# Two matmul orders for a split-weight projection unit: by turns, or all high weights and then all low weights

## The reference

```python
def conv_ffn(h, w_in, conv_w, conv_b, w_out):          # layers 0 and 1, D_FF = 2816
    z = h @ w_in                                       # (256 x 1024) @ (1024 x 5632)
    u, g = z[..., :D_FF], z[..., D_FF:]
    a = causal_dwconv(u, conv_w) + conv_b
    return (jax.nn.silu(a) * g) @ w_out                # (256 x 2816) @ (2816 x 1024)
...
    u = causal_depthwise_conv(xn @ w_up[i], conv_w[i], conv_b[i])   # layer 2
    gate, val = jnp.split(u, 2, axis=-1)
    h = h + (jax.nn.gelu(gate) * val) @ w_down[i]
```

## Time and profile before

| what | value |
|---|---|
| median of 3 executions | 924.18 us (922.28 to 924.61) |
| profiled execution | 926.02 us, span 924.3 us from first to last instruction |
| mean granted TensorE clock | 0.997 of full speed |
| TensorE matmul busy | 909.1 us, 98% of the span |
| VectorE, ScalarE, GpSimd busy | 661.3, 566.3, 245.9 us |
| the kernel's HBM traffic | 179 GB/s over the span |

### The profile page before, as it was taken

One profiled execution on the slowest core, in us unless ns is written; L12 is line 12 of the kernel. 1 busy time (PEld: TensorE's weight loads), 2 busy tenths in 40 slices (PEclk: granted clock), 3 DMA queues, 4 the chain that ended last, 5 costly groups with the idle time before them and its releaser, 6 DMA issues.

```text
span 924.3 us, 18589 instructions
## 1 busy us (share of the span) xinstructions
PE 909.1 (98%) x6182; PEld 826.3 (89%) x6182; DVE 661.3 (72%) x1324; ACT 566.3 (61%) x978; POOL 245.9 (27%) x132
## 2 busy tenths in 40 slices
PE   8999999999999999999999999999999999999996
PEld 8899888888899999988888889999899888898996
DVE  6887887777555766788777866787557776676566
ACT  7356776675445556577666554666558877764453
POOL 2220444430000002034444000250203988840000
PEclk9999999999999999999999999999999999999998
DMA  7556865568534443466556654354334655575521
GB/s 276 172 185 208 237 204 186 190 206 278 180 126 137 138 138 138 139 226 204 186 196 208 226 189 146 106 178 137 115 114 162 223 184 192 193 233 202 180 93 46
DMA packets 46331, 163.53 MB, mean 177 GB/s; under 512 B 5011, under 2 KB 9619, under 8 KB 46278
## 3 DMA queue, kind: packets, MB, share of 16 engines
q1 hardware_dynamic: 41704, 158.19, 51.4%
q10 hardware_dynamic: 4573, 4.62, 1.7%
HBM read 161.71 MB, written 3.44 MB: 179 GB/s over the span
## 4 chain that ended last, share of the span: by engine, by line
PE 90%; DVE 5%; ACT 2%; issue 1%; DMA 1%; SPq 0%; DVEq 0%
PE psum L1414 35%; PE psum L1415 18%; PE psum L1438 9%; PE psum L1439 9%; PE psum L1440 9%; PE psum L1561 2%; PE psum L1563 2%; PE psum L1564 2%; DVE wl L890 1%; PE psum L1673 1%; DMA raw<-in_even_in 1%; ACT wh L549 1%; PE psum L1648 1%; PE psum L1634 1%; PE psum L1612 1%
## 5 line engine op out<-in xcount | busy, mean ns | idle before, releaser
L549 ACT ACTIVATE wh<-raw 128x1024 fp32r<-128x1024 f32 (+2 forms) x270 | 301.4, 1119 | 138.0 <-PE psum L1415 62.9
L1414 PE MATMUL psum<-xs,wh 128*128 128x512 f32 x1024 | 358.4, 396 | 0.0
L485 POOL TENSOR_TENSOR wl<-raw,wh 128x1024 fp32r<-128x1024 f32 (+1 forms) x88 | 214.0, 2436 | 459.5 <-ACT wh L549 458.0
L890 DVE TENSOR_TENSOR wl<-raw,wh 128x1024 fp32r<-128x1024 f32 (+2 forms) x182 | 244.3, 1347 | 59.3 <-ACT wh L549 59.1
L1415 PE MATMUL psum<-xs,wl 128*128 128x256 f32 x1024 | 285.1, 278 | 0.0
L1414 PEld LDWEIGHTS psum<-xs,wh 128*128 128x128 f32 x1024 | 192.2, 188 | 45.9 <-issue 0.3
L1415 PEld LDWEIGHTS psum<-xs,wl 128*128 128x128 f32 x1024 | 192.7, 188 | 0.1
L1438 PE MATMUL psum<-xs,wh 128*128 128x256 f32 x480 | 138.8, 289 | 5.1 <-DVE work L1002 2.5
L1414 PE MATMUL psum<-ys,wh 128*128 128x512 f32 x396 | 139.4, 397 | 0.3 <-DVE psum L930 0.3
L1439 PE MATMUL psum<-xs,wh 128*128 128x256 f32 x480 | 135.7, 283 | 0.0
L1440 PE MATMUL psum<-xs,wl 128*128 128x256 f32 x480 | 135.7, 283 | 0.0
(11 more groups left out here) (218 smaller groups left out, 1282.3 us busy)
## 6 DMA issues: line engine op xcount, KB each, us to landing
raw<-in_up SPq DMA_DIRECT2D x132, 512.0 KB, 3.3
raw<-in_down SPq DMA_DIRECT2D x48, 704.0 KB, 4.2
raw<-in_qkv SPq DMA_DIRECT2D x48, 512.0 KB, 3.3
raw<-in_even_in SPq DMA_DIRECT2D x16, 512.0 KB, 4.2
raw<-in_out SPq DMA_DIRECT2D x16, 512.0 KB, 3.2
raw<-in_ple SPq DMA_DIRECT2D x8, 640.0 KB, 3.9
raw<-in_even_out SPq DMA_DIRECT2D x8, 512.0 KB, 3.3
toeplitz_dram<-table_dram ACTq DMA_DIRECT2D x1, 2048.0 KB
```

Source lines behind the costliest of these rows:

```text
L485: nc.gpsimd.tensor_tensor(low, raw[:, s, 0:tiles * P], high.bitcast(f32), ALU.subtract)\
L549: nc.scalar.activation(split_weights(q, s, tiles * P)[0], raw[:, s, 0:tiles * P], ACT.Copy).then_inc(hi_ready, 1)
L890: nc.vector.tensor_tensor(low, raw[:, s, 0:tiles * P], high.bitcast(f32), ALU.subtract).then_inc(lo_ready[s], 1)
L1414: nc.tensor.matmul(bank, wh[:, s, w], inputs(t), start=first, stop=False)
```

## The change

In `wide_unit` the loop over the tiles is split in two. First all matmuls of 512 columns under the high weights, then all of 256 columns under the low weights. The unit waits at its beginning for the bank and for its high weights (`hi_ready`), and for its low weights only between the two loops. The per-tile waits (`ready`) stay with the first loop. The number, the shapes and the operands of the matmuls stay, as does the semaphore at the unit's end; `unit`, which has the three matmuls of 256 columns, is untouched.

```diff
                 if tiles[0] == 0:
-                    pe.wait_ge(lo_ready[s], q + 1)
                     if start and read is not None:
                         pe.wait_ge(bank_read, read)
+                    pe.wait_ge(hi_ready, q * RING + s + 1)
                 for n, t in enumerate(tiles):
                     if ready:
                         ready(t)
-                    first, last = start and n == 0, stop and n == len(tiles) - 1
-                    w = slice(t * P, (t + 1) * P)
-                    nc.tensor.matmul(bank, wh[:, s, w], inputs(t), start=first, stop=False)
-                    done = nc.tensor.matmul(bank[:, SEQ:2 * SEQ], wl[:, s, w], inputs(t)[:, 0, :], start=False, stop=last)
+                    nc.tensor.matmul(bank, wh[:, s, t * P:(t + 1) * P], inputs(t), start=start and n == 0, stop=False)
+                if tiles[0] == 0:
+                    pe.wait_ge(lo_ready[s], q + 1)
+                for n, t in enumerate(tiles):
+                    done = nc.tensor.matmul(bank[:, SEQ:2 * SEQ], wl[:, s, t * P:(t + 1) * P], inputs(t)[:, 0, :], start=False,
+                                            stop=stop and n == len(tiles) - 1)
                 return done
```

## The result

| what | before | after |
|---|---|---|
| median of 22 executions | 924.16 us (922.28 to 926.41) | 925.91 us (924.73 to 928.56) |
| ratio of the times | | 1.0023 (95% interval 1.0016 to 1.0031) |
| profiled execution | 926.02 us | 926.60 us |
| TensorE matmul busy | 909.1 us | 908.8 us |

The change makes the kernel 0.23% slower by the ratio, 2.1 us, and 1.5 to 2.9 us by its interval; the two medians lie 1.75 us apart. I had forecast 0.31% faster. The range held the time, the sign was wrong.

A forecast was written before the change was run, and what follows sets the result against it. TensorE's own matmuls were taken to bound the kernel: 926.02 - 4.1 (pace) + 1.2 (stops) = 923.1 us for the profiled execution, -0.31%, hence 921.3 for the median; 8 in 10 range 914.5 to 930.5.

The forecast's parts named there:

- What bounds the kernel, and the waits: Wide units are bound by the pace of their own matmuls; moving the two weight waits gains nothing and costs zero.
- The few tens of ns that I named for an uncovered wait: At a unit's edge, an extra wait not covered by matmuls in front would cost this, times 164 units.
- The inputs at the start of a phase: Unit 0 of up1 and up2 stops at tile 6 for inputs: 0.6 and 0.8 us, sum about 1.4, taken as 1.2.
- The price of a 512 behind a 512: Inside wide units, 226.7 ns from one 512 to the next, so a pair takes 346.7 ns in either order.
- rival A: Inside wide units, a run of 512s is cheaper, 216 to 223 ns each; 917.5 us in all; chance 0.24.
- rival B: Inside wide units, 512s stay at about 233 ns and 256s at 120, a pair 353; 929.7 us; chance 0.25.
- My sentence on the units' edges: The whole sum would be wrong if steps at units' edges, 256 to 512 in another bank, grew; no size given.
- The gain from the upper level: In up0, down0 and down2, 616 pairs go from 353.3 to 346.7 ns, gaining 4.1 us; the other 804 gain nothing.
- The lower bound of 213 ns: Lowest price for a 512 to 512 step in wide units, read from the plain f32 matmul of 384 columns.
- A's sum with 213 + 120: The cheaper-512s rival with a 512 at the two-pass rate of 213 ns and a 256 at 120: 906 us.
- C: The change does not touch the pace, both levels stay and only the stalls are left: +1.2, 925.4 us; chance 0.16.

The follow-up runs named there:

- lo_wait_first: The changed kernel, but with the wait for the low weights back at the unit's front, ahead of the first matmul: 926.44 us, ratio 1.0024.
- half_load3: The changed kernel, but low matmuls load 64 weight columns, not 128, and the last tile's low product is left out: 900.36 us, one execution.
- groups_of_4: The changed kernel, but units waiting tile by tile for inputs alternate 512s and 256s, other wide units go in groups of four tiles: 927.40 us, ratio 1.0034.

## Why the prediction was wrong

**What bounds the kernel, and the waits.** Right. TensorE stays at 98%, the extra wait costs nothing and the earlier `hi_ready` gains nothing (`lo_wait_first`). The few tens of ns that I named for an uncovered wait are a guess: no run shows such a price.

**The inputs at the start of a phase.** Right in place and kind: stops at tile 6 in up1 and up2, released by L906, none of this kind in up0 or in the down phases. The size was 1.14 us against 1.4 by rows and 1.2 taken. The step from the VectorE result to TensorE's start was the term: I took 0.26 us; here it is 392.34 - 392.29 = 0.05. With 0.05 in both places the rows give 0.4 and 0.6, as measured.

**The price of a 512 behind a 512.** The value taken, 226.7 ns, is the settled one to the digit, and rival A's 216 to 223 and B's 233 are both refuted for it. The Trainium skill's N/2.4 + 2.5 ns ("TensorE: Matmul & The Clock Gate", "Back-to-back issue gap") gives 215.8 and 109.2; the runs have 226.7 and 120, and the measurement decides. That the digit came out is partly luck. I took 13.3 ns for each matmul because 226.7 + 120 is the lower level. But by turns at that level the two prices are others: in down1 a 512 takes 230 and a 256 takes 117, which has the same sum. The line behind the earlier trace rows shows it, 540.24 to 540.47:

```profile
540.47 0.28 PE L1415 MATMUL psum<-ys,wl 128*128 128x256 f32 x1
```

Wrong was to give 226.7 to every 512 of the run. The first five behind a run of 256s take 27 ns more in sum, of which the first two 256s give back 8. So a pair is 349.1 or 348.4, not 346.7: 2.4 and 1.7 ns over the lower level, where I had nothing. Over the 1420 pairs that is 3.1 us. It is rival B's kind of surplus, at about a third of its price. My sentence on the units' edges ("Wrong would be the whole sum if...") had the place but not the form: the steps at the edge itself did not grow, the five behind it did.

**The gain from the upper level.** This is the step that failed and turned the sign: "616 pairs go from 353.3 to 346.7, 4.1 us. The other 804 gain nothing." The 616 went to 349.1 and 348.4 and gained 2.8 us, and the 804 went up to the same values and lost 1.8. So the pace gained about 1.0 us in the profiled execution, not 4.1, and the stops took that back; the measured six stretches say the same, 498.8 before and after. Then I carried the gain to the median by its share, as if every execution had those 616. That execution stood near the top of the 22, and the two later profiles had 396 and 264 such pairs. I had seen that two phases with the same instructions differed in pace, and that the profiled execution was 1.8 us above the median, and drew no conclusion. With the mean of three profiles, 425 pairs, and the measured paces (mean 348.9), the change gains 425 x 4.4 = 1.9 us there and loses 995 x 2.1 = 2.1 on the others: +0.2. With the stops that is +1.3, where the medians have +1.75 and the interval 1.5 to 2.9. The first sum with its terms mended is thus close. The remaining 0.4 us or more is not explained, and from three profiles the mix is known only roughly.

**Slips that did not decide.** The two records in the earlier trace rows are not two matmuls: the program issues L1634 once for each half, and the trace has two records for it. So one plain f32 matmul of 384 columns takes 0.64 us, and each of its records 0.32, the time of 768 columns at 2.4 GHz. How many passes it makes the trace does not say. The lower bound of 213 ns for a 512 in fp32r rests on a matmul of another kind. A's sum with 213 + 120 is 904.6 us by its own terms, not 906. And my own gain was counted over all 1420 pairs, those of the rivals over 1250.

**The rivals.** C gave 925.4 and is nearest (925.91), but not by its mechanism: it had both levels staying, and in the profiles after there is only one pace in each kind of phase. What it had right is that the mean pace hardly moves and that the stops are what is left.

## What to carry over

When two stretches of one profile issue the same instructions at different paces, take more profiles before a gain is counted on either: the level may differ from execution to execution. Where an order is changed in a stream of matmuls, price the passages between shapes and not just the settled steps, and look at what the old order did as filler at places that wait input by input; that filler was here more than half of the 1.75 us. Longer runs of one shape pay only if the results they delay are not due.

## What the runs showed of the hardware

- An fp32r matmul of 512 columns behind others of 512 takes 226.7 ns from start to start at the granted clock of 1.00, one of 256 behind others of 256 takes 120. The difference, 106.7, is 256 columns at 2.4 GHz, which leaves 13.3 ns for each matmul. With 64 columns of weights, and so 64 output channels, the 256 takes 113 (`half_load3`), with 8 columns 117.
- At the granted clock of 0.50 (1.2 GHz) a 256 takes 213 ns from start to start, in `groups_of_4` between 11 and 14 us.
- Passing from 256s to 512s costs 27 ns over the next five, whether the loads ahead were of 128 or 64 columns. Inside the all-512 stretches there is none of it.
- Alternating 512 and 256 runs in one of two steady patterns, 346.7 or 353.3 ns a pair, for a hundred us and more. At the upper level the steps are 232, 118, 241, 120, 236 and 113 ns over and over (`before`, up0), at the lower 230 and 117 (down1), or 231 and 233 by turns with 112 to 118 (up1). Which one holds differs between executions of one program; the cause is open.
- One plain f32 matmul of 384 columns leaves two records in the trace and takes 0.64 us in all.
